# Memory keys in one 512-column pass over both halves of the memory rows, their two sums added by VectorE

## The reference, cut to what matters

```python
def memory_xattn(h, m, wq, wk, wv, wo):
    q = (h @ wq)...
    k = (m @ wk).reshape(B, M, MEM_HEADS, MEM_HEAD_DIM)   # m: 256 normed memory rows of 1024
    v = (m @ wv)...
```

## Time and profile before

| what | value |
|---|---|
| median of 3 runs | 1818.58 us (1818.46 to 1818.71) |
| the profiled execution, its own time | 1819.9 us |
| its span in the trace | 1818.1 us |
| TensorE busy | 1805.1 us, 99% of the span |
| VectorE busy | 1314.0 us, 72% |
| ScalarE busy | 1049.6 us, 58% |
| granted TensorE clock | 1.00 of full speed, the higher of its two levels, all through |

### The profile page before, as it was taken

One profiled execution on the slowest core, in us unless ns is written; L12 is line 12 of the kernel. 1 busy time (PEld: TensorE's weight loads), 2 busy tenths in 40 slices (PEclk: granted clock), 3 DMA queues, 4 the chain that ended last, 5 costly groups with the idle time before them and its releaser, 6 DMA issues.

```text
span 1818.1 us, 26710 instructions
## 1 busy us (share of the span) xinstructions
PE 1805.1 (99%) x10324; PEld 1548.6 (85%) x10324; DVE 1314.0 (72%) x1712; ACT 1049.6 (58%) x1519; POOL 238.7 (13%) x261
## 2 busy tenths in 40 slices
PE   9999999999999999999999999999999999999998
PEld 7888999788888888889987888888888889888887
DVE  6776777876766776677688677667787667797665
ACT  5655545765654565555466665556675455675443
POOL 2010122010100011003021000002101111301110
PEclk9999999999999999999999999999999999999999
DMA  9686663363656567766345356555447554645661
GB/s 317 201 281 203 166 203 128 119 214 119 221 196 194 177 208 237 247 175 204 131 140 189 125 189 217 180 193 164 174 140 231 186 190 165 232 131 187 197 192 70
DMA packets 227793, 337.91 MB, mean 186 GB/s; under 512 B 22519, under 2 KB 172177, under 8 KB 227410
## 3 DMA queue, kind: packets, MB, share of 16 engines
q1 hardware_dynamic: 220178, 307.06, 51.9%
q0 software_dynamic: 7488, 29.14, 4.8%
HBM read 335.13 MB, written 1.05 MB: 185 GB/s over the span
## 4 chain that ended last, share of the span: by engine, by line
PE 90%; DVE 6%; ACT 2%; issue 1%; DMA 0%; SPq 0%; POOL 0%; DVEq 0%; ACTq 0%
PE ps L1797 87%; PE ps L1802 3%; DVE wlo L1173 3%; ACT whi L725 1%; ACT region L725 1%; DVE region L1173 1%; DVE xn L1173 1%; DVE region L1181 0%; DMA xs<-x 0%; DVE xs L1181 0%; DVE mlo L1173 0%; DVE ahl L1173 0%; DVE sm L1189 0%; ACT mhi L725 0%; DVE sm L1177 0%
## 5 line engine op out<-in xcount | busy, mean ns | idle before, releaser
L1173 DVE TENSOR_TENSOR wlo<-raw,whi 128x1024 fp32r<-128x1024 f32 (+1 forms) x456 | 565.8, 1241 | 173.5 <-ACT whi L725 137.6
L725 ACT ACTIVATE whi<-raw 128x1024 fp32r<-128x1024 f32 (+1 forms) x456 | 479.9, 1052 | 76.3 <-PE ps L1797 28.6
L1797 PE MATMUL ps<-ahl,whi 128*128 128x512 f32 (+1 forms) x1824 | 415.9, 356 | 1.3 <-DVE rmb L1185 1.3
L1797 PEld LDWEIGHTS ps<-ahl,whi 128*128 128x128 f32 x1824 | 316.4, 189 | 44.3 <-DVE rmb L1185 1.7
L725 ACT ACTIVATE region<-ps 128x512 f32<-128x512 f32 (+2 forms) x268 | 155.8, 582 | 279.2 <-PE ps L1797 224.7
L1797 PE MATMUL ps<-whi,ahl 128*128 128x512 f32 (+2 forms) x944 | 300.0, 385 | 1.1 <-DVE wlo L1173 1.1
L1797 PE MATMUL ps<-ahl,wlo 128*128 128x256 f32 x1520 | 255.5, 282 | 0.0
L1797 PEld LDWEIGHTS ps<-ahl,wlo 128*128 128x128 f32 x1520 | 224.1, 191 | 11.9
L1797 PEld LDWEIGHTS ps<-whi,ahl 128*128 128x128 f32 x944 | 174.3, 188 | 36.3 <-DVE wlo L1173 1.7
L1173 DVE TENSOR_TENSOR mlo<-raw,mhi 128x1024 fp32r<-128x1024 f32 (+2 forms) x132 | 163.3, 1237 | 45.3 <-ACT mhi L725 34.9
L555 POOL TENSOR_TENSOR hlo<-region,hhi 128x512 fp32r<-128x512 f32 x62 | 81.7, 1318 | 793.7 <-ACT hhi L725 793.7
(11 more groups left out here) (176 smaller groups left out, 2359.6 us busy)
## 6 DMA issues: line engine op xcount, KB each, us to landing
raw<-w_ff SPq DMA_DIRECT2D x64, 1024.0 KB, 5.4
raw<-ffn_w_down SPq DMA_DIRECT2D x44, 1024.0 KB, 5.0
raw<-ffn_w_gate SPq DMA_DIRECT2D x40, 1024.0 KB, 5.2
raw<-ffn_w_up SPq DMA_DIRECT2D x40, 1024.0 KB, 5.7
raw<-w_in SPq DMA_DIRECT2D x34, 1024.0 KB, 5.4
raw<-w_out SPq DMA_DIRECT2D x16, 1024.0 KB, 4.9
raw<-xa_wk SPq DMA_DIRECT2D x8, 1024.0 KB, 5.1
raw<-xa_wv SPq DMA_DIRECT2D x8, 1024.0 KB, 5.1
```

The source lines that it names most:

```text
L725: e.activation(o, i, f, **kw).then_inc(*act.did(*names))
L1173: e.tensor_tensor(o, a, b, op).then_inc(*dve.did(*names))
L1797: m = e.matmul(o, l, r, start=start, stop=stop)
```

## The change

The two halves of the memory rows move into one tile MHL, in which each block of depth has 256 columns of the high half and then 256 of the low half. A key piece becomes eight matmuls of 512 columns (both halves by `whi`) and eight of 256 columns (the high half by `wlo`). The bank then holds two sums: columns 0 to 255 have high by high plus high by low, columns 256 to 511 low by high. ScalarE copies columns 256 to 511 to `mkT`, and VectorE adds columns 0 to 255 to it (`memory_sum`). What waited for ScalarE's copy of a key piece waits for VectorE's addition now.

```diff
-        MHI = sb("mhi", 8 * T, F32R)
-        MLO = sb("mlo", 8 * T, F32R)
+        MHL = sb("mhl", 16 * T, F32R)
...
-                    put(mkT[:, p * 256:(p + 1) * 256], PS[:, (3, 1)[p % 2], 0:256], ACT.Copy, ("memory", l, p))
+                    put(mkT[:, p * 256:(p + 1) * 256], PS[:, (3, 1)[p % 2], 256:512], ACT.Copy, ("memory", l, p))
...
+                def memory_sum(p):
+                    k = mkT[:, p * 256:(p + 1) * 256]
+                    q.wait_ge(*act.at("memory", l, p))
+                    tt(k, k, PS[:, (3, 1)[p % 2], 0:256], ALU.add, ("memory_sum", l, p))
...
                     if u < 7:
                         maximum(u + 1)
+                    if u < 4:
+                        memory_sum(2 * u)
                     if u == 3:
                         take(s, *HSPLIT[2], 0)
...
                     weight(u)
+                    if u < 4:
+                        memory_sum(2 * u + 1)
...
                     if p >= 2:
-                        q.wait_ge(*act.at("memory", l, p - 2))
+                        q.wait_ge(*dve.at("memory_sum", l, p - 2))
...
-                    up_tile(hi, lo, f, (3, 1)[f], 0, mhv, mlv, ("memory", l, p), *([("used", i)] if f else []))
+                    bank, c = (3, 1)[f], slice(f * 128, (f + 1) * 128)
+                    for k in range(8):
+                        mm(PS[:, bank, :], hi[:, k, c], mhl[:, k, :], k == 0, False)
+                    for k in range(8):
+                        end = (("memory", l, p), *([("used", i)] if f else [])) if k == 7 else ()
+                        mm(PS[:, bank, 0:256], lo[:, k, c], mhl[:, k, 0:256], False, k == 7, *end)
...
                     if u == 3:
-                        q.wait_ge(*act.at("memory", l, 5))
+                        q.wait_ge(*dve.at("memory_sum", l, 5))
                         blocks(s + 0.5, 1, 1, 1)
```

More of the change, by code:

```diff
@@ L458, in build @@
         homes = [(WHI[:, i * 2048:(i + 1) * 2048], WLO[:, i * 2048:(i + 1) * 2048]) for i in range(NSPLIT)]
-        homes.append((MHI[:, :], MLO[:, :]))
+        homes.append((MHL[:, 0:8 * T], MHL[:, 8 * T:16 * T]))
         gains = gain_rows(A)
@@ L489, in build @@
         ahv, alv = axv[:, :, 0:T], axv[:, :, T:2 * T]
-        mhv, mlv = [x[:, :].rearrange("p (k n) -> p k n", k=8) for x in (MHI, MLO)]
+        mhl = MHL[:, :].rearrange("p (k n) -> p k n", k=8)
+        mhv, mlv = mhl[:, :, 0:T], mhl[:, :, T:2 * T]
         hhv, hlv = [[x[:, :].rearrange("p (k n) -> p k n", k=2) for x in y] for y in (HH, HL)]
@@ L2090, in memory_piece @@
                 elif c == 0:
-                    q.wait_ge(*act.at("memory", l, 6 if p == 8 else p - 1))
+                    q.wait_ge(*(dve.at("memory_sum", l, 6) if p == 8 else act.at("memory", l, p - 1)))
                 ms = slice(m * 128, (m + 1) * 128)
@@ L2260, in hybrid @@
                         if u == 4 and k == 1:
-                            q.wait_ge(*act.at("memory", l, 7))
+                            q.wait_ge(*dve.at("memory_sum", l, 7))
                         for i in range(4):
```

## The result

| | before | after |
|---|---|---|
| median | 1818.58 us (5 runs, 1818.46 to 1818.71) | 1826.59 us (5 runs, 1826.03 to 1826.77) |
| ratio | | 1.0043, 95% interval 1.0030 to 1.0056 |
| the profiled execution: its time, its span | 1819.9 us, 1818.1 us | 1826.74 us, 1824.9 us |

The kernel became slower by 8.0 us. The prediction was 1826.8 us, that is 8.2 us more.

What follows compares the result with a forecast made beforehand. TensorE was taken to bound the kernel, with VectorE nearly full in the key-piece stretch. Additions on VectorE delay TensorE 4.1 us a layer, 8.2 us in all, on 1818.6: 1826.8 us, range 1822.0 to 1830.0 us.

Steps and rivals of the forecast that it cites:

- 1. maximum of unit 2; piece 4: Additions of pieces 0 and 1 delay VectorE's maximum by 1.0 us; piece 4, waiting for piece 2's addition, is 1.2 late.
- 2. ScalarE's group with the copy of piece 3 (310.89 before): This copy, behind unit 2's exponentials, is 1.0 us late; VectorE is then 2.1 us late after piece 3's addition.
- 3. maximum of unit 3; blocks of unit 3: Maximum 2.1 us late, so ScalarE's copy and VectorE's addition of piece 5 hold TensorE's activation blocks 2.6 us late.
- 4. scores of unit 4; piece 8: VectorE's scores 2.5 us late; with piece 6's addition the `wv` 0 split holds piece 8 by 2.8 us.
- 5. copy of piece 7; split of `wv` 1; piece 9: Copy 2.6 us late; piece 7's addition waits for it ahead of the split; VectorE 5.1 us late, piece 9 3.6.
- 6. maximum of unit 5; copy of piece 9; piece 10: Maximum and ScalarE's copy 5.1 us late; piece 10 waits for that copy in bank 3, 4.1 us late.
- 7. scores behind it (335.42 before), then level: VectorE's 0.91 us wait cuts its lateness from 5.1 to 4.2 us, level with TensorE; no further loss behind piece 10.
- The rival of the direct waits alone: TensorE loses only 2.8 us a layer, VectorE's longer lateness finds room: 1824.2 us; chance 0.22.
- The rival in which VectorE's whole lateness stays: TensorE takes over 5.1 us a layer or more, with no room at 335.42: 1828.8 us; chance 0.15.
- The bound of 0.26 us for GpSimd's work: If GpSimd slows VectorE beside it, 0.26 us more on each of unit 0's two additions, 0.5 us a layer.
- The rival of hidden additions: VectorE's 4.3 us of free time in the stretch takes the additions; only fewer matmuls count: 1817.3 us; chance 0.09.
- The rival of the weight loads: Weight loads set TensorE's pace, so eight fewer a piece save 24 us at most: 1803 us; chance 0.02.

Runs made afterwards that it cites:

- e2: Changed kernel with the old narrow matmuls; VectorE does a maximum of the same shape in place of each addition: 1826.73 us.
- e6: The change for key pieces 0 to 3 alone, pieces 4 to 7 as in the kernel before: 1822.32 us.
- e7: Changed kernel with VectorE's addition of piece 7 moved behind its split of `wv` 1: 1823.62 us.
- e12: Changed kernel with ScalarE's copies of pieces 1, 3, 5 and 7 moved ahead of the exponentials: 1822.97 us.
- e4: The change in layer 1 alone, layer 0 with the pieces of before: 1822.11 us.
- e1: Changed kernel's wide matmuls without additions; ScalarE copies columns 0 to 255, low-by-high sums left out of the keys: 1818.69 us.
- e9: e1 with VectorE's reduction in unit 0 cut to 8 of 128 columns, 1.0 us less work: 1816.86 us.
- e10: Kernel before with VectorE's reduction in unit 0 cut to 8 of 128 columns, 1.0 us less work: 1818.01 us.
- e3: e2 with VectorE's operations cut to 8 of 256 columns, all waits kept: 1823.64 us.
- e11: Changed kernel with VectorE's reduction in unit 0 cut to 8 of 128 columns, 1.0 us less work: 1825.80 us.
- e8: Changed kernel's matmuls, but ScalarE copies both sums and GpSimd adds them instead of VectorE: 1822.39 us.

## Why the prediction was right

The forecast held: slower, by 8.0 us where 8.2 were forecast, in the two stretches that it named and with the releasers that it named. Its steps, with the lateness of layer 0 (distance from piece 0, after less before):

| step | predicted, us | measured, us |
|---|---|---|
| 1. maximum of unit 2; piece 4 | 1.0; 1.2 | 0.88; 1.13 |
| 2. ScalarE's group with the copy of piece 3 (310.89 before) | 1.0 | 0.87 |
| 3. maximum of unit 3; blocks of unit 3 | 2.1; 2.6 | 1.77; 2.35 |
| 4. scores of unit 4; piece 8 | 2.5; 2.8 | 2.30; 2.56 |
| 5. copy of piece 7; split of `wv` 1; piece 9 | 2.6; 5.1; 3.6 | 2.22; 4.69; 3.15 |
| 6. maximum of unit 5; copy of piece 9; piece 10 | 5.1; 5.1; 4.1 | 4.62; 4.61; 3.62 |
| 7. scores behind it (335.42 before), then level | 4.2 | 3.80 |

- *Steps 1 to 4, the direct waits*, are shown by e2 (the additions alone give all of it) and by e6 (half of it without the additions of pieces 4 to 7). Step 1 left one stop out: piece 2 waits 0.46 us for the addition of piece 0, as it writes that bank. It costs nothing on top, since piece 4 waits for VectorE anyway.
- *Steps 5 and 6, the addition of piece 7 that holds the split of `wv` 1 for a copy*, are shown twice, by e7 and by e12: with the addition behind the split, or with the copy earlier, the stops at pieces 9 and 10 go and the distance falls by 1.3 us. The rival of the direct waits alone, 1824.2 us, lacked just these; e7 and e12 at 1823.6 and 1823.0 us are about that rival's kernel.
- *Step 7* is shown by the row at 338.49 (the 0.91 us are used up), and by e4: a layer's loss stays in that layer. The rival in which VectorE's whole lateness stays falls with it. "No further loss" was not quite so: in layer 0 the transposes behind piece 12 start 349.82 - 338.21 = 11.61 us behind piece 10, against 346.69 - 335.32 = 11.37 before, and the trace names ScalarE as their releaser, so the lateness of VectorE (3.80 us) and ScalarE was still a little more than TensorE's 3.62 us. This is 0.24 of the 0.28 us that layer 0 loses behind piece 10; in layer 1 the same place loses nothing.
- *The mis-sized term* is the lateness per addition in steps 1 to 3. Two of them put the maximum of a unit later by 0.88 us, not by 1.0 in unit 0 and 1.1 in unit 1. The split behind the odd one got shorter, since its wait for ScalarE moved to the addition: 2.48 us at 304.06 in unit 0, against 2.60 at 303.81 before, and 2.48 against 2.55 us in unit 1. There the copy for which the addition of piece 3 waits was late by 0.87 us and not by 1.0. This makes 0.3 us at unit 3, and the later steps carried it on, to 0.5 us at piece 10. The bound of 0.26 us for GpSimd's work beside the additions of unit 0 was not needed. By the rows the one at 300.88 ran when no GpSimd instruction did, and the one at 303.61 beside one (303.17, 1.67 us); both lasted 0.42 us.
- *The sum* came nearer than its parts: 3.62 + 3.46 = 7.1 us in the two stretches against 8.2. The rest of the 8.0 us lies in about 0.5 us between and behind them, for which the prediction had no term, and in the difference of the profiled executions; the interval of the ratio, 5.5 to 10.2 us, doesn't tell these apart. That 8.0 came within 0.2 us of 8.2 is therefore in part luck; the mechanism is what held.
- *The rival of hidden additions* gave 1817.3 us and rested on two things, both of which the runs refute: VectorE's free time doesn't take the additions (e2), and without any additions the kernel isn't faster (e1). The prediction's argument against this rival misread where that free time lies: of the 4.33 us in the earlier trace rows, 1.01 lie ahead of 294.01 and 0.62 at 318.44, and the other 2.7 us are gaps of under 0.15 us between VectorE's instructions, in which no addition fits. The prediction had said that the 1.3 us come "if TensorE never waits"; e1 and e9 show that it waits as soon as it gets ahead, and that the 1.3 us come, as 1.15, when VectorE has 1 us of room.
- *The rival of the weight loads* is refuted by e9 against e10: 64 loads fewer in a layer gave 0.54 us there, 0.008 us each, where a load's row has 0.188. The rule of the Trainium skill ("TensorE: Matmul & The Clock Gate", Back-to-back issue gap), that weight load and matmul together set the spacing, does not show in this kernel; its loads lie beside the matmuls.

One thing stays open. In e3, additions of 0.16 us still cost 2.26 us a layer; how this splits between waits for ScalarE and the bank's longer hold was not measured apart. A kernel with both e7's and e12's moves wasn't run either; as both take away the same two stops, I expect the 2.96 us of the other four to remain in it.

## What to carry to other kernels

Before work is moved to an engine that is "72% busy", read in the stretch itself what its results are early by; here the split was 0.26 us early, and a 0.42 us addition couldn't hide. When a result that one engine used to finish takes two, look at what stands ahead of the first engine's part and behind the second's part in their queues: in a ring between two engines that work strictly in order, the order can cost as much as the work. Moving one addition a layer (e7) gave back 3.0 of 8.0 us and moving four copies a layer (e12) 3.6, with no work taken away. Taking 1.0 us of work off VectorE ahead of a wait (e11) gave 0.2 us a layer, as it only made the wait longer, while shortening the additions themselves (e3) gave 3.1 us. And a saving on the engine that bounds the kernel is a saving only if those that feed it have room; 1.15 us of matmul time were worth nothing until VectorE had 1 us of room.

## What the runs showed of the hardware that was not expected

- An addition of 8 columns with an operand in PSUM lasts 0.16 us on VectorE, one of 256 columns 0.42 us: 0.26 us for 248 columns, about 1 ns each; by a straight line through these two, an estimate, 0.15 us do not depend on the columns.
- In e8, GpSimd took 0.72 to 0.79 us for seven of the eight additions of a layer (256 columns, two operands in SBUF), 1.7 to 1.9 times VectorE's 0.42 us with one operand in PSUM. The eighth, that of piece 1, took 1.54 us in layer 0 (304.10) and 1.53 in layer 1; why was not tested.
- The one addition of layer 0 on VectorE that ran beside a GpSimd instruction kept its 0.42 us (303.61), while the small scaling at 300.35, beside another, took 0.43 us against 0.17 elsewhere. Whether GpSimd is the cause of that was not tested.
- A split of two halves on VectorE took 2.48 us where neither half had a wait for ScalarE in front of it and 2.55 us where the second one had, without a bracket for it in the row: 0.07 us more, all of it between the halves.
